# Two more rooms for the first expert table in batches 19 to 28

## The chip, the cores and the metric

The kernel runs on one core of a Trainium2 chip, in one launch. The metric is device time in microseconds (us). The kernel before was timed three times: 2976.99, 2976.50 and 2975.83 us, median 2976.5 us. The profile comes from one further execution.

## The reference, cut to what matters

Two transformer layers run over 256 tokens with 2048 features in float32; the change touches only the last part of the second, a layer of single-neuron experts (`peer`). Each token picks, for each of 8 heads, 16 of 16384 experts, and computes

```
u = jnp.take(expert_u, idx, axis=0)
a = jnp.einsum('thkd,td->thk', u, xb)
hid = jax.nn.gelu(a) * g
vsel = jnp.take(expert_v, idx, axis=0)
return jnp.einsum('thk,thkd->td', hid, vsel)
```

So there is a row of the first table (`expert_u`) to take, a dot product with the token's activations `xb`, a gate, and a row of the second table (`expert_v`) to add, 128 times for each token.

## The kernel before, in words

**Sparse and dense experts.** Of the 128 blocks of 128 experts, the last 40 are computed densely: their rows come as 40 panels of each table, 1 MB each, and TensorE multiplies all tokens by them (first table: `dense_u_panel`, second table: `dense_v_panel`). The other 88 blocks are sparse: their rows are gathered by index; an index that points into the dense blocks is out of bounds and moves no row.

**Gathers and rooms.** One gather takes 128 rows, one for each token of a half of the tokens, into a tile of 128 x 2048 floats (1 MB if no row were left out). There are 256 gathers of each table, numbered k = 0 to 255; four make a batch g = k // 4, 64 batches in all. Batches 0 to 31 serve the first 128 tokens, batches 32 to 63 the late rows (tokens 128 to 255). A tile of the first table goes into a room `s_u`, of the second table into a room `s_v`. There are 5 and 7 rooms; from batch 34 (`WIDE`) on 7 and 8. GpSimd (POOL) issues all gathers from one queue in one order: `gather_u(k)`, then `gather_v(k - 4)`. `gather_u(k)` waits until the last tile in its room has been used by a dot product (`dot_ready`), and `gather_v(k)` until TensorE has added the last tile in its room (`v_used`). Since the queue is in order, a gather that waits holds back all behind it.

**The other engines.** VectorE (DVE) computes `dot(k)`, two instructions on a room `s_u`. ScalarE (ACT) makes the gelu and the small matrices `s_spread`, and TensorE (PE) adds batch g's four `s_v` tiles (`adds`) one batch later. The first table's dense panels run on TensorE in batches 0 to 17, the last of them (panel 39) at the end of step 17. In steps 18 to 31, TensorE computes the gates of the dense experts, four tokens at a time (`token_four`, 64 of them: 8 each in steps 18 and 19, 4 each in 20 to 31), which counts `one_key_used`. The second table's dense panels run in steps 34 and later.

**The panel buffers.** Panels come through `s_raw0` and `s_raw1`, 8 KB per partition each, by DMAs that SyncE (SP) issues. Behind the last panel of the first table SP loads `s_xn_late` and `s_xres_late` (the late rows' activations and residual, 1 MB each, first needed in batch 32 and step 33), and then the first two panels of the second table (needed in step 34). Each of these waits for a count of `one_key_used`: 4, 8, 12 and 16. So between panel 39 and the second table's first panels, `s_raw0` and `s_raw1` hold nothing for a short time and then those panels.

Of the kernel before, what the change touches and what calls it, by code (L numbers as in the profile page):

```python
# [22 lines left out]
D = 2048  # L23
# [10 lines left out]
PH, TOPK, NKEYS = 8, 16, 128  # L34
SLOTS = PH * TOPK

DENSE = 40
# [9 lines left out]
NPANELS = sum(n for _, n in PANELS)  # L47
# [91 lines left out]
def four_of(g):  # L139

    if g < 4 * EARLY:
        return g % EARLY, g // EARLY
    if g < 4 * PH:
        g -= 4 * EARLY
        return EARLY + g % (PH - EARLY), g // (PH - EARLY)
    g -= 4 * PH
    return PH + g % PH, g // PH
# [38 lines left out]


WIDE = 34


def rooms_of(narrow, wide, start, tiles):

    rooms = []
    last, times = {}, [0] * wide
    later = list(range(narrow, wide)) + [(start + i) % narrow for i in range(narrow)]
    for k in range(tiles):
        r = k % narrow if k < start else later[(k - start) % wide]
        times[r] += 1
        rooms.append((r, times[r], last.get(r)))
        last[r] = k  # L200
    return rooms
# [42 lines left out]
def two_layers(nc, stream, dense_u, columns, x, meta, b_out, g_mix_post, g_ffn, g_ffn_post, g_norm1, g_norm2, w_forget,  # L244
# [5 lines left out]
    K, Q = 1024, 32  # L250
# [3 lines left out]
    def place(name, shape, offset, dt=f32):  # L254
        assert name not in names
        names.add(name)
        return nc.alloc_sbuf_tensor_at(name, shape, dt, offset=offset)
# [29 lines left out]
    ring0 = at  # L287
# [5 lines left out]
    S = at  # L293
# [60 lines left out]
    NE = len(panel_early)  # L354
    score = place("s_score", [128, TT * PH, 2 * NKEYS], S + 16 * K)
    NU, NV, NW, NH, BATCH, LAG = 5, 7, 4, 4, 4, 4
    ROUTES, GROUPS = TT * PH, TOPK // BATCH
    MU, MV = NU + 2, NV + 1
    u_room = rooms_of(NU, MU, WIDE * BATCH, ROUTES * TOPK)
    v_room = rooms_of(NV, MV, WIDE * BATCH, ROUTES * TOPK)  # L360


    ha = place("s_ha", [128, DENSE, T], S + 24 * K)
    u_slot = [place(f"s_u{i}", [128, D], before_group if i == 0 else ring0 + (1 + i) * 8 * K) for i in range(NU)]
    u_slot += [place("s_u5", [128, D], S + 0), place("s_u6", [128, D], S + 16 * K)]
    free = [S + 8 * K, ring0 - 8 * K, ring0 + 48 * K, ring0 + 56 * K, ring0 + 64 * K + (KT * L * 4),
            ring0 + 72 * K + (KT * L * 4), ring0 - 16 * K]
    v_slot = [place(f"s_v{i}", [128, D], free[i]) for i in range(NV)]
# [51 lines left out]
    with ExitStack() as ctx:  # L420
        bank = [ctx.enter_context(nc.psum_tensor(f"bank{b}", [128, 512], f32)) for b in range(8)]

        def sem(name):
            return ctx.enter_context(nc.semaphore(name))
# [5 lines left out]
        panel_used = sem("panel_used")  # L430
# [41 lines left out]
        one_key_ready, one_key_2_ready, one_key_used = sem("one_key_ready"), sem("one_key_2_ready"), sem("one_key_used")  # L472
# [6 lines left out]
        dot_ready, dots_added, gelu_ready, hid_ready = sem("dot_ready"), sem("dots_added"), sem("gelu_ready"), sem("hid_ready")  # L479
# [15 lines left out]
        @block.sync  # L495
        def _(sp):
            sp.dma_start(meta_sb[:, :], meta).then_inc(meta_loaded, 16)
            for t in range(TT):
                sp.dma_start(xres[:, t, :], x[t * 128:(t + 1) * 128, :]).then_inc(x_loaded[t], 16)
            sp.dma_start(cols[:, :], columns).then_inc(cols_loaded, 16)  # L500
            for s in range(4):
                sp.dma_start(raw[s][:, :], stream[s]).then_inc(raw_loaded[s], 16)
            panels = stream.rearrange("(q s) p n -> q s p n", s=4)
            with sp.Fori(1, NPANELS // 4) as q:
                for s in range(4):


                    sp.wait_ge(panel_used, q * 4 + (s - 4 + 1 + 1))
                    sp.dma_start(raw[s][:, :], panels[bass.ds(q, 1), s].rearrange("a p n -> (a p) n"))\
                        .then_inc(raw_loaded[s], 16)  # L510
            for d in range(NE, 2 * DENSE):
                if d == DENSE:
                    sp.wait_ge(panel_used, NPANELS + 1 + DENSE)
                    sp.wait_ge(one_key_used, 4)
                    sp.dma_start(xn_late[:, :], put_by[0]).then_inc(xn_back, 16)
                    sp.wait_ge(one_key_used, 8)
                    sp.dma_start(xres_late[:, :], put_by[1]).then_inc(xres_back, 16)
                if DENSE <= d < DENSE + 2:
                    sp.wait_ge(one_key_used, 12 + 4 * (d - DENSE))
                if d < NE + 2:  # L520
                    sp.wait_ge(split_ready, NSPLITS - 3 + d - NE)
                else:
                    sp.wait_ge(panel_used, NPANELS + 1 + d + 1 - 2)
                src = dense_u[d] if d < DENSE else expert_v[(SPARSE + d - DENSE) * NKEYS:(SPARSE + d - DENSE + 1) * NKEYS, :]
                r = (d - NE) % 2
                sp.dma_start(raw[r][:, :], src).then_inc(raw_loaded[r], 16)
            for t in range(TT):
                for q in range(4):
                    sp.wait_ge(out_ready, 4 * t + q + 1)
                    for c in range(4 if t == 0 else 2):  # L530
                        sp.dma_start(out[t * 128 + q * Q:t * 128 + (q + 1) * Q, c * 512:(c + 1) * 512],
                                     out_row[c * Q:(c + 1) * Q, t, q * 512:(q + 1) * 512]).then_inc(stored, 16)
            sp.wait_ge(stored, 16 * 16 * TT)
# [3 lines left out]
        def _(pool):  # L537
# [51 lines left out]
            for g, w in enumerate(POOL_WINDOWS):  # L589
                src, s = pin[:, 2 * g:2 * g + 2, :], 1  # L590
                own = src
# [28 lines left out]
            def gather_u(k):  # L620

                g, s = divmod(k, BATCH)
                th, j = four_of(g)
                slot = j * BATCH + s
                pool.wait_ge(expert_ready, th + 1)
                if k in (1, 2):
                    pool.wait_ge(split_ready, NSPLITS - 2 + k)
                if k in (3, 4):
                    pool.wait_ge(panel_used, NPANELS - 3 + k)
                r, _, last = u_room[k]  # L630
                if last is not None:
                    pool.wait_ge(dot_ready, last + 1)
                elif r == NU:
                    pool.wait_ge(dot_ready, PH * GROUPS * BATCH)
                elif r > NU:
                    pool.wait_ge(one_key_used, T // 4)
                index = bass.IndirectOffsetOnAxis(ap=u_index[th][:, slot:slot + 1], axis=0)
                pool.indirect_dma_start(u_slot[r][:, :], None, expert_u, index, bounds_check=SPARSE * NKEYS - 1,  # L638
                                        oob_is_err=False).then_inc(u_loaded[r], 16)

            def gather_v(k):

                g, q = divmod(k, BATCH)
                th, j = four_of(g)
                pool.wait_ge(v_index_ready, th + 1)
                if k == 0:
                    pool.wait_ge(late_stored, 32)
                if k == 4:
                    pool.wait_ge(xnt_ready, 1)
                if k == 6:  # L650
                    pool.wait_ge(res_taken, 1)
                r, _, last = v_room[k]
                if last is not None:
                    pool.wait_ge(v_used, last + 1)
                elif r >= NV:
                    pool.wait_ge(v_used, PH * GROUPS * BATCH + 1)
                index = bass.IndirectOffsetOnAxis(ap=v_index[th][:, q * GROUPS + j:q * GROUPS + j + 1], axis=0)
                pool.indirect_dma_start(v_slot[r][:, :], None, expert_v, index, bounds_check=SPARSE * NKEYS - 1,  # L658
                                        oob_is_err=False).then_inc(v_loaded[r], 16)

            gather_u(0)
            gather_v(0)
            gather_v(1)
            for k in range(1, ROUTES * TOPK + LAG):
                if k < ROUTES * TOPK:
                    gather_u(k)
                for first in {4: (2, 3), 5: (4, 5), 6: (6,)}.get(k, ()):
                    gather_v(first)
                if k >= LAG + NV:
                    gather_v(k - LAG)  # L670
# [1856 lines left out]
```

## Time and profile before

| | |
|---|---|
| median of three runs | 2976.5 us |
| the profiled execution's own time | 2973.8 us |
| its span in the profile | 2971.7 us |
| busy: TensorE, VectorE, ScalarE, GpSimd | 2759.5, 1917.5, 1177.4, 660.7 us |
| granted TensorE clock, mean | 0.948 of full speed |
| DMA, mean over the span | 264 GB/s |
| batches 0 to 63: first dot product to the last | 1851.1 to 2958.5 us |
| first dot product on the late rows (k = 128) | 2415.3 us |

The gathers fill the last 1100 us of the span. In the page's 40 slices (74.3 us each) the DMA engines are busy at 50 to 60% until then and at over 90% from slice 26 on. Times given as a place are counted from the start of the span.

### The profile page before, as it was taken

What the parts mean: (1) busy time and instruction counts of PE and PEld (TensorE: products, weight loads), DVE (VectorE), ACT (ScalarE), POOL (GpSimd) and SP (SyncE); (2) the same over time, 40 slices, a digit from 0 to 9 for tenths busy, and PEclk for the clock granted to TensorE, in tenths of its full rate; (3) what the DMA queues carried; (4) which work ended last, traced back from release to release, by engine and by line L of the source; (5) the groups of instructions that cost most, each with busy time, mean ns of one, the idle gap of its engine ahead of it and who ended that gap; (6) DMA issues with size and microseconds to landing.
All of it is one profiled execution on the core that took longest, in us unless ns stands there. A gap on an engine that the chain in (4) does not pass through costs nothing.

```text
span 2971.7 us, 45765 instructions
## 1 busy us (share of the span) xinstructions
PE 2759.5 (93%) x17115; PEld 2063.2 (69%) x17115; DVE 1917.5 (65%) x3302; ACT 1177.4 (40%) x2302; POOL 660.7 (22%) x568
## 2 busy tenths in 40 slices
PE   8999999999999997999999999999998787888885
PEld 7886778888888887989999889677764432222221
DVE  6888566655665556455444557988858885555556
ACT  1003443333333434434333445565556542223333
POOL 0000000000000000040000002454446665555554
PEclk9999999999999998999999999999996679989897
DMA  6432545555555553443455656999999999999998
GB/s 246 142 142 101 209 158 187 193 186 183 189 192 183 186 193 121 165 147 141 173 185 184 249 201 226 365 409 416 413 378 419 401 409 423 423 422 420 419 420 356
DMA packets 131299, 785.53 MB, mean 264 GB/s; under 512 B 34630, under 2 KB 34630, under 8 KB 35846
## 3 DMA queue, kind: packets, MB, share of 16 engines
q1 hardware_dynamic: 55040, 393.16, 36.0%
q0 software_dynamic: 75712, 389.74, 32.4%
q8 instruction: 94, 1.54, 0.2%
q14 instruction: 69, 0.57, 0.1%
q10 hardware_dynamic: 384, 0.52, 0.0%
HBM read 940.23 MB, written 4.19 MB: 318 GB/s over the span
## 4 chain that ended last, share of the span: by engine, by line
PE 62%; DMA 16%; DVE 12%; issue 6%; ACT 2%; POOL 2%; DVEq 1%; POOLq 0%; ACTq 0%
PE bank L1970 10%; PE bank L1964 10%; PE bank L1965 10%; PE bank L1966 10%; DMA s_u<-in_expert_u,s_u_index 10%; DMA s_v<-in_expert_v,s_v_index 6%; PE bank L2363 6%; PE bank L1971 5%; PE bank L2060 4%; DVE s_u L1824 3%; PE bank L2418 3%; PE bank L2373 2%; DVE s_cacc L1333 2%; POOL s_u L638 1%; DVE s_w_lo L1244 1%
## 5 line engine op out<-in xcount | busy, mean ns | idle before, releaser
L1244 DVE TENSOR_TENSOR s_w_lo<-s_raw,s_w_hi 128x2048 fp32r<-128x2048 f32 x258 | 592.6, 2297 | 577.0 <-ACT s_w_hi L685 576.5
L685 ACT ACTIVATE s_w_hi<-s_raw 128x2048 fp32r<-128x2048 f32 x256 | 490.4, 1916 | 750.6 <-PE bank L1966 475.2
L1970 PE MATMUL bank<-s_a,s_w_hi 128*128 128x512 f32 x1408 | 494.3, 394 | 3.2 <-DVE s_w_lo L1244 3.2
L1824 DVE CUSTOM_DVE_ANT_0 s_u<-s_u,s_xn_late 128x1024 f32<-128x1024 f32 x256 | 303.6, 1223 | 221.2 <-DMA s_u<-in_expert_u,s_u_index 195.3
L2418 PE MATMUL bank<-s_v,s_spread 128*32 128x512 f32 x2048 | 312.5, 727 | 142.2 <-DMA s_v<-in_expert_v,s_v_index 106.0
L1971 PE MATMUL bank<-s_a,s_w_lo 128*128 128x256 f32 x1408 | 395.1, 281 | 0.0
L638 POOL DMA_INDIRECT s_u<-in_expert_u,s_u_index x256 | 298.9, 1168 | 381.4 <-DVE s_halfdot L1824 222.4
L658 POOL DMA_INDIRECT s_v<-in_expert_v,s_v_index x256 | 311.5, 1217 | 206.6 <-PE bank L2418 120.3
L1824 DVE CUSTOM_DVE_ANT_0 s_u<-s_u,s_xn 128x1024 f32<-128x1024 f32 x256 | 303.0, 1223 | 46.6 <-DMA s_u<-in_expert_u,s_u_index 40.9
L1964 PE MATMUL bank<-s_a,s_w_hi 128*128 128x256 f32 x1152 | 325.1, 282 | 3.4 <-DVE s_a L1268 1.8
L1965 PE MATMUL bank<-s_a,s_w_hi 128*128 128x256 f32 x1152 | 324.4, 282 | 0.0
L1966 PE MATMUL bank<-s_a,s_w_lo 128*128 128x256 f32 x1152 | 324.0, 281 | 0.0
L1109 ACT ACTIVATE s_spread<-s_shifted,s_hid 32x32 f32<-32x32 f32 x784 | 249.4, 318 | 188.0 <-DVE s_hid L1873 169.0
L1970 PEld LDWEIGHTS bank<-s_a,s_w_hi 128*128 128x128 f32 x1408 | 264.7, 188 | 66.2 <-DVE s_w_lo L1244 6.4
L2418 PEld LDWEIGHTS bank<-s_v,s_spread 128*32 128x32 f32 x2048 | 64.0, 123 | 341.0 <-issue 284.6
L2373 PE MATMUL bank<-s_raw,s_ha 128*32 128x512 f32 x2560 | 297.1, 617 | 0.0
L2363 PE MATMUL bank<-s_xnt,s_raw 128*128 128x256 f32 x1184 | 265.2, 382 | 1.3 <-issue 0.9
L1971 PEld LDWEIGHTS bank<-s_a,s_w_lo 128*128 128x128 f32 x1408 | 264.9, 188 | 0.4
L2363 PEld LDWEIGHTS bank<-s_xnt,s_raw 128*128 128x128 f32 x1184 | 221.9, 190 | 59.6 <-issue 30.9
L2060 PE MATMUL bank<-s_a_f,s_raw 128*128 128x272 f32 x1024 | 235.2, 393 | 2.0 <-DVE s_a_f L1301 1.2
L2373 PEld LDWEIGHTS bank<-s_raw,s_ha 128*32 128x32 f32 x2560 | 94.8, 115 | 202.8 <-issue 202.0
L2060 PEld LDWEIGHTS bank<-s_a_f,s_raw 128*128 128x128 f32 x1024 | 194.4, 190 | 42.6 <-issue 2.6
(332 smaller groups left out, 3912.3 us busy)
## 6 DMA issues: line engine op xcount, KB each, us to landing
s_raw<-in_stream SPq DMA_DIRECT2D x292, 1024.0 KB, 4.8
s_raw<-in_expert_v SPq DMA_DIRECT2D x40, 1024.0 KB
s_raw<-in_dense_u SPq DMA_DIRECT2D x37, 1024.0 KB
s_u<-in_expert_u,s_u_index POOLq DMA_INDIRECT x256
s_v<-in_expert_v,s_v_index POOLq DMA_INDIRECT x256
s_panel_early<-in_dense_u POOLq DMA_DIRECT2D x3, 1024.0 KB, 11.4
s_xres<-in_x SPq DMA_DIRECT2D x2, 1024.0 KB, 5.9
out<-s_out_row SPq DMA_DIRECT2D x24, 64.0 KB
```

Source lines behind the costliest of these rows:

```text
L685: act.activation(w_hi[s % 2][:, :], raw[s][:, :], ACT.Copy).then_inc(hi_ready, 1)
L1244: dve.tensor_tensor(w_lo[s % 2][:, :], raw[s][:, :], w_hi[s % 2][:, :].bitcast(f32), ALU.subtract)\
L1824: ins = dve.tensor_tensor_reduce(out=u_slot[r][:, half], in0=u_slot[r][:, half], in1=xn_late[:, half] if t else xn[:, 0, half], scale=SHRI ...
L1964: pe.matmul(dst, left[0], right[0], start=start, stop=False)
L1965: pe.matmul(dst, left[0], right[1], start=False, stop=False)
L1966: return pe.matmul(dst, left[1], right[0], start=False, stop=stop)
L1970: pe.matmul(dst, left[0], both, start=start, stop=False)
L1971: return pe.matmul(dst[:, 0:T], left[1], both[:, 0], start=False, stop=stop)
L2060: ins = pe.matmul(bank[c][:, 0:L], raw[c % 4][:, k * 128:(k + 1) * 128], a_f[:, k, :], start=k == 0, stop=k == KT - 1)
L2363: ins = pe.matmul(bank[b][:, 0:T], source[:, k * 128:(k + 1) * 128], xnt[:, k, 0:T], start=k == 0, stop=k == KT - 1)
L2373: ins = pe.matmul(bank[4 * t + q][c * Q:(c + 1) * Q, :], ha[:, d, t * 128 + q * Q:t * 128 + (q + 1) * Q], raw[r][:, c * 512:(c + 1) * 512] ...
L2418: ins = pe.matmul(bank[4 * t + q][c * Q:(c + 1) * Q, :], spread[g % NW][:, q, :], v_slot[r][:, c * 512:(c + 1) * 512], start=False, stop=last)
```

## The change

`LENT = (19, 29)`: in batches 19 to 28 (k = 76 to 115) the first table has seven rooms. The two new ones, `s_u5` and `s_u6`, are the bytes of `s_raw0` and `s_raw1`. The two rooms that it has from batch 34 on are now called `s_u7` and `s_u8`. `rooms_of` now takes the open room whose last use is longest ago. The first gathers into the lent rooms, k = 76 and 77, wait until the first table's last dense panel is used (`panel_used`). On SP's queue the load of `s_xn_late` now waits for 24 groups of four tokens in place of 4, that of `s_xres_late` for 32 in place of 8, and the second table's first two dense panels wait for the last dot product in the lent rooms (k = 112 and 111) in place of 12 and 16 groups. The last gathers into the lent rooms are k = 111 and 112. Nothing is computed in another way or in another order on TensorE, VectorE or ScalarE.

```diff
+LENT = (19, 29)
-def rooms_of(narrow, wide, start, tiles):
+def rooms_of(stages, tiles):
     rooms = []
-    last, times = {}, [0] * wide
-    later = list(range(narrow, wide)) + [(start + i) % narrow for i in range(narrow)]
+    last, times = {}, {}
     for k in range(tiles):
-        r = k % narrow if k < start else later[(k - start) % wide]
-        times[r] += 1
+        open_rooms = [own for start, own in stages if start <= k][-1]
+        r = min(open_rooms, key=lambda own: last.get(own, -1))
+        times[r] = times.get(r, 0) + 1
         rooms.append((r, times[r], last.get(r)))
         last[r] = k
...
-    MU, MV = NU + 2, NV + 1
+    MU, MV = NU + 4, NV + 1
+    narrow = list(range(NU))
+    u_room = rooms_of([(0, narrow), (LENT[0] * BATCH, [NU, NU + 1] + narrow), (LENT[1] * BATCH, narrow),
+                       (WIDE * BATCH, [NU + 2, NU + 3] + narrow)], ROUTES * TOPK)
+    lent_until = [max(k for k in range(ROUTES * TOPK) if u_room[k][0] == NU + r) for r in range(2)]
...
+    u_slot += [place("s_u5", [128, D], ring0), place("s_u6", [128, D], ring0 + 8 * K)]
...
                 if d == DENSE:
                     sp.wait_ge(panel_used, NPANELS + 1 + DENSE)
-                    sp.wait_ge(one_key_used, 4)
+                    sp.wait_ge(one_key_used, 24)
                     sp.dma_start(xn_late[:, :], put_by[0]).then_inc(xn_back, 16)
-                    sp.wait_ge(one_key_used, 8)
+                    sp.wait_ge(one_key_used, 32)
                     sp.dma_start(xres_late[:, :], put_by[1]).then_inc(xres_back, 16)
                 if DENSE <= d < DENSE + 2:
-                    sp.wait_ge(one_key_used, 12 + 4 * (d - DENSE))
+                    sp.wait_ge(dot_ready, lent_until[(d - NE) % 2] + 1)
...
                 if last is not None:
                     pool.wait_ge(dot_ready, last + 1)
-                elif r == NU:
+                elif r in (NU, NU + 1):
+                    pool.wait_ge(panel_used, NPANELS + 1 + DENSE)
+                elif r == NU + 2:
```

GpSimd's queue at the start of batch 19, before: k = 75 of the first table (room 0, `s_u_133`), then k = 76 to 78 in rooms 1 to 3, with the second table's gathers between.

```order
L638 DMA s_u_133<-in_expert_u,s_u_index_187 128x2048 [waits dot_ready,expert_ready]
L658 DMA s_v_141<-in_expert_v,s_v_index_202 128x2048 [waits v_used,v_index_ready]
L638 DMA s_u_134<-in_expert_u,s_u_index_188 128x2048 [waits dot_ready,expert_ready]
L658 DMA s_v_142<-in_expert_v,s_v_index_203 128x2048 [waits v_used,v_index_ready]
L638 DMA s_u_135<-in_expert_u,s_u_index_188 128x2048 [waits dot_ready,expert_ready]
L658 DMA s_v_143<-in_expert_v,s_v_index_203 128x2048 [waits v_used,v_index_ready]
L638 DMA s_u_136<-in_expert_u,s_u_index_188 128x2048 [waits dot_ready,expert_ready]
```

The same place of the changed kernel, where `s_u_138` and `s_u_139` are the lent rooms.

```order
L645 DMA s_u_133<-in_expert_u,s_u_index_189 128x2048 [waits dot_ready,expert_ready]
L665 DMA s_v_143<-in_expert_v,s_v_index_204 128x2048 [waits v_used,v_index_ready]
L645 DMA s_u_138<-in_expert_u,s_u_index_190 128x2048 [waits panel_used,expert_ready]
L665 DMA s_v_144<-in_expert_v,s_v_index_205 128x2048 [waits v_used,v_index_ready]
L645 DMA s_u_139<-in_expert_u,s_u_index_190 128x2048 [waits panel_used,expert_ready]
L665 DMA s_v_145<-in_expert_v,s_v_index_205 128x2048 [waits v_used,v_index_ready]
L645 DMA s_u_134<-in_expert_u,s_u_index_190 128x2048 [waits dot_ready,expert_ready]
```

The order of tables is the same; k = 76 and 77 go to the lent rooms and wait for the dense panels, and k = 78 takes the room that k = 76 had.

SyncE's queue behind the first table's last panel, before: the late rows, then the second table's panels.

```order
L515 DMA s_xn_late<-put_by 128x2048 [waits one_key_used,panel_used]
L517 DMA s_xres_late<-put_by 128x2048 [waits one_key_used]
L526 DMA s_raw_66<-in_expert_v 128x2048 [waits panel_used,one_key_used]
L526 DMA s_raw_65<-in_expert_v 128x2048 [waits panel_used,one_key_used]
L526 DMA s_raw_66<-in_expert_v 128x2048 [waits panel_used]
```

The same place after.

```order
L520 DMA s_xn_late<-put_by 128x2048 [waits one_key_used,panel_used]
L522 DMA s_xres_late<-put_by 128x2048 [waits one_key_used]
L531 DMA s_raw_66<-in_expert_v 128x2048 [waits panel_used,dot_ready]
L531 DMA s_raw_65<-in_expert_v 128x2048 [waits panel_used,dot_ready]
L531 DMA s_raw_66<-in_expert_v 128x2048 [waits panel_used]
```

The order of the loads is the same; the two panels now wait for dot products.

## Rows read from the trace of the kernel before

**Rows 1.** The page: rate in each of 40 slices; the gathers' queue (packets, MB, share).

```profile
GB/s 246 142 142 101 209 158 187 193 186 183 189 192 183 186 193 121 165 147 141 173 185 184 249 201 226 365 409 416 413 378 419 401 409 423 423 422 420 419 420 356
...
q0 software_dynamic: 75712, 389.74, 32.4%
```

**Rows 2.** Windows: stretch, its length, busy us of PE, PEld, DVE, ACT, POOL; clock; DMA share; GB/s.

```profile
2200.00:2210.00 10.00, 8.49 (x48) 6.18 (x40) 4.37 (x11) 7.38 (x22) 5.28 (x5) 1.00 0.87 313
2210.00:2230.00 20.00, 17.98 (x114) 13.21 (x114) 13.50 (x27) 15.60 (x49) 8.98 (x8) 0.74 0.94 334
2230.00:2260.00 30.00, 23.88 (x152) 14.08 (x156) 27.07 (x57) 21.39 (x65) 17.99 (x16) 0.73 1.01 417
...
2290.00:2325.00 35.00, 27.67 (x154) 13.25 (x154) 29.63 (x58) 20.60 (x62) 25.42 (x20) 0.69 1.01 411
2325.00:2345.00 20.00, 18.42 (x106) 12.18 (x106) 17.09 (x36) 11.89 (x38) 12.08 (x12) 0.66 0.99 372
...
2370.00:2390.00 20.00, 18.21 (x106) 11.98 (x98) 17.19 (x34) 13.29 (x41) 13.37 (x12) 0.67 0.98 377
...
2440.00:2925.00 485.00, 406.07 (x3452) 122.76 (x3448) 275.28 (x559) 148.27 (x476) 267.32 (x226) 0.91 1.01 420
```

**Rows 3.** Windows of L638 alone (first table's gathers): busy (count), clock, share, GB/s.

```profile
1800.00:2201.00 401.00, 83.19 (x76) 1.00 0.95 378
```

**Rows 4.** The same of L1824 alone (dots, four records each).

```profile
1850.00:2357.00 507.00, 268.22 (x452) 0.91 0.99 397
```

**Rows 5.** Timeline of SyncE, 2180 to 2480: start, us, what.

```profile
2218.22 0.33 SPq L515 DMA_DIRECT2D s_xn_late<-put_by  x1
2228.17 0.33 SPq L517 DMA_DIRECT2D s_xres_late<-put_by  x1
2235.41 237.95 SPq L526 DMA_DIRECT2D s_raw<-in_expert_v  x5
```

**Rows 6.** Timeline of GpSimd; in brackets the idle time before and its releaser.

```profile
2199.70 1.63 POOL L658 DMA_INDIRECT s_v<-in_expert_v,s_v_index  x1 [6.97 <-PE bank L2418]
2201.63 0.99 POOL L638 DMA_INDIRECT s_u<-in_expert_u,s_u_index  x1 [0.30 <-PE bank L2418]
2202.93 0.99 POOL L658 DMA_INDIRECT s_v<-in_expert_v,s_v_index  x1 [0.30 <-issue]
2204.22 0.99 POOL L638 DMA_INDIRECT s_u<-in_expert_u,s_u_index  x1 [0.30 <-issue]
...
2220.89 1.07 POOL L658 DMA_INDIRECT s_v<-in_expert_v,s_v_index  x1 [6.05 <-PE bank L2418]
...
2238.13 1.11 POOL L658 DMA_INDIRECT s_v<-in_expert_v,s_v_index  x1 [2.38 <-DVE s_halfdot L1824]
...
2248.59 1.15 POOL L638 DMA_INDIRECT s_u<-in_expert_u,s_u_index  x1 [3.73 <-DVE s_halfdot L1824]
```

**Rows 7.** Timeline of TensorE: last dense panel, adds, fours of tokens.

```profile
2201.32 7.17 PE L2363 MATMUL bank<-s_xnt,s_raw 128*128 128x256 f32 x32
...
2235.31 5.93 PE L2418 MATMUL bank<-s_v,s_spread 128*32 128x512 f32 x32
...
2267.74 1.96 PE L2398 MATMUL bank<-s_one_key,s_one_key_more 128*128 128x40 f32 x16
...
2298.17 1.96 PE L2398 MATMUL bank<-s_one_key,s_one_key 128*128 128x40 f32 x16
```

**Rows 8.** Waits on GpSimd, 2180 to 2420: us in total, times, longest.

```profile
POOL s_u L638 <- DVE s_halfdot L1824: 37.8, 20, 4.0
...
POOL s_v L658 <- PE bank L2418: 13.3, 3, 7.0
```

**Rows 9.** Chain of waits, 2120 to 2480: gathers from issue to landing.

```profile
2261.11 12.96 DMA s_u<-in_expert_u,s_u_index
...
2374.32 14.59 DMA s_u<-in_expert_u,s_u_index
```

More of the change, by code:

```diff
@@ L357, in two_layers @@
     ROUTES, GROUPS = TT * PH, TOPK // BATCH
-    MU, MV = NU + 2, NV + 1
-    u_room = rooms_of(NU, MU, WIDE * BATCH, ROUTES * TOPK)
-    v_room = rooms_of(NV, MV, WIDE * BATCH, ROUTES * TOPK)
+    MU, MV = NU + 4, NV + 1
+    narrow = list(range(NU))
+    u_room = rooms_of([(0, narrow), (LENT[0] * BATCH, [NU, NU + 1] + narrow), (LENT[1] * BATCH, narrow),
+                       (WIDE * BATCH, [NU + 2, NU + 3] + narrow)], ROUTES * TOPK)
+    v_room = rooms_of([(0, list(range(NV))), (WIDE * BATCH, [NV] + list(range(NV)))], ROUTES * TOPK)
+    lent_until = [max(k for k in range(ROUTES * TOPK) if u_room[k][0] == NU + r) for r in range(2)]
     ha = place("s_ha", [128, DENSE, T], S + 24 * K)
     u_slot = [place(f"s_u{i}", [128, D], before_group if i == 0 else ring0 + (1 + i) * 8 * K) for i in range(NU)]
-    u_slot += [place("s_u5", [128, D], S + 0), place("s_u6", [128, D], S + 16 * K)]
+    u_slot += [place("s_u5", [128, D], ring0), place("s_u6", [128, D], ring0 + 8 * K)]
+    u_slot += [place("s_u7", [128, D], S + 0), place("s_u8", [128, D], S + 16 * K)]
     free = [S + 8 * K, ring0 - 8 * K, ring0 + 48 * K, ring0 + 56 * K, ring0 + 64 * K + (KT * L * 4),
@@ L632, in gather_u @@
                     pool.wait_ge(dot_ready, last + 1)
-                elif r == NU:
+                elif r in (NU, NU + 1):
+                    pool.wait_ge(panel_used, NPANELS + 1 + DENSE)
+                elif r == NU + 2:
                     pool.wait_ge(dot_ready, PH * GROUPS * BATCH)
-                elif r > NU:
+                elif r == NU + 3:
                     pool.wait_ge(one_key_used, T // 4)
```

## The prediction

> **What bounds the kernel now.** I read the page's slices first. From slice 26 on the DMA engines move 401 to 423 GB/s in nearly every slice, against 101 to 250 in the first 25 [rows 1]. Then I cut that stretch into windows. From 2440 to 2925 us the rate is 420 GB/s at a share of 1.01: there DMA bandwidth is the bound, and what is left to move at 2440 sets the end [rows 2]. Before 2440 there are two kinds of shortfall. From 2200 to 2230 the rate is 313 and 334 GB/s; this is where TensorE finishes the last dense panel and does double portions of token groups. From 2260 on it is near 420 but for two holes, 2325 to 2345 (372) and 2370 to 2390 (377), and a slight one at 2290 to 2325 (411) [rows 2]. So the account to keep is one of megabytes: every microsecond in which the engines move less than 420 GB/s before 2440 is paid at the end.
>
> Shortfall against 420 GB/s, in us: 2200 to 2210, 107/420 x 10 = 2.5; 2210 to 2230, 86/420 x 20 = 4.1; 2230 to 2260, 0.2; 2290 to 2325, 0.75; 2325 to 2345, 2.3; 2370 to 2390, 2.05. That is 6.8 us in the first part and 5.1 us in the later one: 11.9 us is all that a better supply of gathers could win.
>
> Why are there holes? GpSimd's queue waits for a free room. Between 2180 and 2420 it waited 37.8 us for dot products, that is for rooms of the first table, 20 times, and 13.3 us, 3 times, for rooms of the second [rows 8]. Two of those three are 6.97 us before 2199.70 and 6.05 us before 2220.89, 13.0 us together [rows 6], so from 2221 on the second table's rooms are named for hardly any wait.
>
> **The unit.** The gathers' queue moved 389.74 MB [rows 1]. Thirteen direct loads of 1.05 MB and a small one went by it too, so 512 gathers share some 376 MB: 0.734 MB each, 1.75 us at 420 GB/s. A panel or a late load is 1.05 MB, 2.5 us.
>
> **The waits at the start of the loan.** 76 gathers of the first table were issued before 2201 [rows 3], so k = 76 is the one at 2201.63 [rows 6]. It now waits for the last dense panel, which TensorE computes from 2201.32 for 7.17 us, to 2208.5 [rows 7]. Queued behind it are the second table's k = 72, the first's k = 77 and the second's k = 73, issued at 2202.93 and 2204.22 and after. All move back to about 2208.8, by 7 us. The next fixed point is the second table's gather at 2220.89, which waits for TensorE's adds of step 18, and the next the one at 2238.13 (its releaser is named as a dot product, but the adds of step 19 start at 2235.31 and fit as well) [rows 6, 7]. Between these the queue has room: 7 gathers at 1.3 us each fit between 2208.8 and 2218. So the 7 us are made up on GpSimd by 2221; the DMA engines meanwhile have one or two gathers left and run dry.
>
> **The loads that move.** Before, the two late loads went out at 2218.22 and 2228.17 and the second table's first panels from 2235.41 on (12 and 16 groups of tokens) [rows 5]; they filled the weak stretch. Now `s_xn_late` waits for the 24th group, done at 2267.74 + 1.96 = 2269.7, and `s_xres_late` for the 32nd, at 2300.1 [rows 7]. The two panels wait for dot product k = 112: 452 records at four each are 113 dot products by 2357 [rows 4]. All are in time for batch 32 and step 34, which start after 2415. So 4 x 1.05 = 4.2 MB, 10.0 us of DMA time, move from a stretch with slack into one with little.
>
> **What is delivered by 2260.** Before: 10 us x 313 + 20 x 334 + 30 x 417 = 22.3 MB, the 4.2 MB included [rows 2]. After: no more than was issued can arrive by 2239.6, and the fixed point at 2238.13 holds back the same second-table gathers as before. These are 8 of the first table (76 to 83) and 7 of the second (72 to 78), 15 x 0.734 = 11.0 MB, and 1.1 MB in flight at 2200, an estimate. From 2239.6 to 2260 GpSimd can issue one gather per 1.3 us, since the next wait for a dot product (3.73 us before 2248.59 [rows 6]) is for two products earlier now; so 20.4 us at 420 = 8.6 MB. Sum 20.7 MB, 1.6 MB less than before: **3.8 us lost**. Bounds: 10.0 us if no extra gather takes the place of the moved loads, and 0 if TensorE and VectorE, with less traffic beside them, free the rooms so that the weak stretch is filled as before.
>
> **What the two rooms give from 2260 on.** GpSimd is some 3 to 4 gathers ahead at 2260, and it has 7 rooms until k = 115 (some 2355). The slight shortfall (0.75) and the hole at 2325 (2.3) should close: 3.05 us. At the hole of 2370 the first table is back at five rooms, but 2.1 MB of panels, 5.0 us of work, were issued at 2357; I credit half of it, 1.0 us. **About 4.0 us gained**, between 0 and 5.1. VectorE does not stand against it: it is busy 29.63 of 35 us at 2290 [rows 2]. The new names of the rooms from batch 34 on cost nothing, since order and number are the same.
>
> The sum: 2973.8 (the profiled execution, 2.1 us around its span of 2971.7) + 3.8 - 4.0 = 2973.6. That execution stands 2.7 us under the median of the runs, so the forecast is 2976.3, rounded to 2976.0: **no change**.
>
> [...] In the hole the rate is 377 GB/s while a gather takes 14.59 us from issue to landing [rows 2, 9]; 14.59 us x 377 GB/s is 5.5 MB, 7.5 gathers in flight of the 12 rooms, and the engines are still not full. At 2261.11 it is 12.96 us [rows 9]. [...]
>
> **Rivals.**
> *The second table's rooms take over.* Slower. Place: GpSimd's `v_used` waits from batch 20 on. A gather of the second table stands between any two of the first, its seven rooms are as they were, and its tile is used one batch later. If GpSimd, once ahead, always stops there, gathers are delivered as before and the 4.2 MB are pure addition to the stretch 2260 to 2440: +10.0 us, less what of them falls into the holes (2 to 5.1 us): +5 to +8, 2981.5 to 2984.5. It decides as soon as those waits in 2240 to 2350 exceed some 10 us. For it: 13.3 us of such waits before. Against: none of weight after 2221 [rows 6, 8].
> *Depth buys nothing.* The holes come from GpSimd's and VectorE's pace and stay: +3.8, 2980.3. Against: 37.8 us of waits for dot products.
> *The weak stretch is filled after all.* Faster: of 11.9 us of shortfall all but the dry 4 us at 2201 goes: -8, 2968.5. For it: half of the shortfall lies there. Against: the fixed points at 2220.89 and 2238.13 are no rooms of the first table.
> *The loan does nothing and neither do the moved loads*: within 1 us; it can't be told from the forecast by the time, only by the waits.
>
> **How the numbers follow.** A measurement of this kernel tells 0.2% (6 us) from no change. Forecast 0.46, depth buys nothing 0.18, second table's rooms 0.18, weak stretch filled 0.18. The forecast's own range is 2972 to 2980. Beyond the 6 us lie most of the third and of the fourth case: slower 0.15, faster 0.16, same 0.69. The range runs from 2970 to 2983, which leaves the outer ends of both, 2 in 10.
>
> **What would show it.** Right: GpSimd idle for 6 to 7 us up to 2208.8 before k = 76, with DMA under 200 GB/s there; `s_xn_late` issued near 2270, `s_xres_late` near 2300, both panels near 2350; rates of 415 and more from 2290 to 2345; fewer waits of GpSimd for dot products in 2240 to 2360. Wrong: waits for TensorE's adds of 10 us or more there (second table's rooms), holes in the same places (depth), or dot product k = 128 earlier than 2415 by over 5 us with the same rate after 2440 (faster). A shift of more than 3 us that arises behind 2440 would break the account as such.

## The result, and the profile after

| | median, us | runs | against the kernel before in the same set |
|---|---|---|---|
| before | 2974.9 | 22 | |
| changed | 2979.78 | 22 | ratio 1.0016, 95% interval 1.001 to 1.0022; 4.9 us slower |

The forecast was 2976.0 us and no change. The time lies inside the range of 2970 to 2983 us, but the change is slower by more than its interval: small, under the 6 us that the prediction called the limit of what can be told, and told all the same by 22 runs of each kernel. The first three runs of the kernel before, on which the forecast stood, have a median of 2976.5 us; all 22 have 2974.9 us, so beside these the forecast itself stood 1.6 us too high. The profiled execution of the changed kernel took 2984.28 us, the longest of its 22; its first dot product starts at 1853.7 us, 2.6 us later than before, ahead of everything that was changed. All windows below are moved by such an offset (here 2.6 us), so that they begin as far behind the first dot product as those of before; where a view is not moved, the text says so.

The page of the changed kernel, GB/s in 40 slices and the gathers' queue; the same bytes as before [rows 1].

```profile
GB/s 246 141 142 99 204 163 185 191 188 183 190 190 184 190 188 127 159 152 139 176 183 183 240 201 238 371 409 414 413 358 406 409 402 423 423 421 420 418 417 350
...
q0 software_dynamic: 75712, 389.74, 32.3%
```

Windows of the kernel before, for all comparisons below (stretch, length, busy us of PE, PEld, DVE, ACT, POOL, clock, DMA share, GB/s). The stretch ahead of them, 2200 to 2210, and the one behind, from 2440, stand in [rows 2].

```profile
2210.00:2260.00 50.00, 41.87 (x264) 27.30 (x268) 40.57 (x83) 36.99 (x113) 26.97 (x24) 0.73 0.98 384
2290.00:2345.00 55.00, 46.09 (x260) 25.43 (x260) 46.72 (x93) 32.49 (x100) 37.50 (x31) 0.68 1.00 397
2345.00:2440.00 95.00, 71.20 (x418) 34.06 (x421) 76.74 (x149) 46.41 (x143) 62.86 (x54) 0.70 1.01 409
```

The same of the changed kernel, with the stretch ahead and the one behind.

```profile
2202.60:2212.60 10.00, 8.66 (x48) 6.26 (x40) 3.76 (x8) 7.38 (x22) 1.34 (x2) 1.00 0.38 144
2212.60:2262.60 50.00, 41.18 (x268) 26.82 (x272) 41.44 (x84) 37.96 (x115) 35.09 (x29) 0.74 0.95 365
2292.60:2347.60 55.00, 42.49 (x248) 23.32 (x241) 44.88 (x91) 32.31 (x100) 37.47 (x29) 0.69 1.01 412
2347.60:2442.60 95.00, 72.06 (x418) 36.24 (x418) 73.58 (x145) 44.13 (x136) 59.33 (x49) 0.67 1.00 401
2442.60:2927.60 485.00, 405.62 (x3444) 120.68 (x3440) 275.00 (x556) 144.90 (x467) 264.74 (x226) 0.90 1.01 420
```

Read as a shortfall against 420 GB/s (the rate of the last stretch, unchanged), in us, (420 - rate) / 420 x length. The four stretches are called A (2200 to 2210), B (2210 to 2260), C (2290 to 2345) and D (2345 to 2440); between B and C both kernels run at 423 GB/s:

| | A | B | C | D | sum |
|---|---|---|---|---|---|
| before | 2.5 | 4.3 | 3.0 | 2.5 | 12.3 |
| changed | 6.6 | 6.5 | 1.0 | 4.3 | 18.4 |

Up to 2260 the change costs 6.3 us. The two rooms win 2.0 us in C, and 1.8 us of that is gone in D. The sum is 6.1 us more, beside 4.9 us between the medians. The two profiled executions themselves lie 10.5 us apart, or 7.9 us without the 2.6 us at the start.

What stands in A: GpSimd's timeline of the changed kernel, with the idle time before each gather and its releaser. L665 is the second table's gather, L645 the first's, L2370 TensorE's dense panel.

```profile
2202.46 0.99 POOL L665 DMA_INDIRECT s_v<-in_expert_v,s_v_index  x1 [10.80 <-PE bank L2425]
2212.11 0.99 POOL L645 DMA_INDIRECT s_u<-in_expert_u,s_u_index  x1 [8.66 <-PE bank L2370]
2213.41 1.75 POOL L665 DMA_INDIRECT s_v<-in_expert_v,s_v_index  x1 [0.30 <-issue]
```

The gather k = 76 waits 8.66 us for the last dense panel, as the change says, where it had gone out 0.30 us behind its neighbour [rows 6]. Ahead of it the queue had waited 10.80 us for the adds, so that in 21 us one gather was issued, and the DMA engines ran at 144 GB/s. The 10.80 us are not the change's: two kernels below without loan or added wait show 10.55 and 10.35 us in this place, and A is at 334 and 341 GB/s in them. What empties A is the second wait on top.

SyncE's timeline of the changed kernel:

```profile
2271.37 0.33 SPq L520 DMA_DIRECT2D s_xn_late<-put_by  x1
2301.40 0.33 SPq L522 DMA_DIRECT2D s_xres_late<-put_by  x1
2360.53 129.59 SPq L531 DMA_DIRECT2D s_raw<-in_expert_v  x6
```

The late rows' loads went out at 2218.22 and 2228.17 before, the panels from 2235.41 [rows 5]. Now none of the four falls into B.

Waits on GpSimd from 2240 to 2360 in both kernels (not moved by the offset), before and then changed.

```profile
POOL s_u L638 <- DVE s_halfdot L1824: 14.4, 8, 3.7
...
POOL s_v L658 <- DVE s_halfdot L1824: 2.1, 1, 2.1
```

```profile
POOL s_v L665 <- PE bank L2425: 12.9, 3, 6.9
...
POOL s_v L665 <- DVE s_halfdot L1831: 6.6, 4, 5.6
...
POOL s_u L645 <- DVE s_halfdot L1831: 0.6, 2, 0.3
```

One of these waits, 5.6 us ahead of the gather at 2240.34, has its counterpart before ahead of the one at 2238.13, outside the view. With the window moved by 2.6 us the changed kernel's 6.6 us are 0.9. So the wait has changed its owner: 14.4 us for the first table's rooms became 0.6, and 2.1 us at the second table's gathers became 13.8 (12.9 + 0.9). The deeper side no longer waits; the other one does, for about as long.

### The profile page after: what moved, and what is told of

It is laid out like the page before. It is cut to its first block, busy times and chain, and to the rows that moved or that the text cites. A ratio compares the mean times of both kernels' runs of the same rounds, so it can differ in the third digit from the quotient of the medians.

```text
span 2982.2 us, 45765 instructions
## 1 busy us (share of the span) xinstructions
PE 2760.3 (93%) x17115; PEld 2063.4 (69%) x17115; DVE 1916.2 (64%) x3302; ACT 1177.5 (39%) x2302; POOL 662.9 (22%) x568
## 4 chain that ended last, share of the span: by engine, by line
PE 62%; DMA 17%; DVE 12%; issue 5%; ACT 2%; POOL 1%; DVEq 1%; POOLq 0%; SPq 0%; ACTq 0%
PE bank L1977 10%; PE bank L1971 10%; PE bank L1972 10%; PE bank L1973 10%; DMA s_u<-in_expert_u,s_u_index 9%; DMA s_v<-in_expert_v,s_v_index 8%; PE bank L2370 5%; PE bank L1978 5%; PE bank L2067 4%; DVE s_u L1831 3%; PE bank L2425 3%; DVE s_cacc L1340 1%; PE bank L2380 1%; PE bank L2405 1%; DVE s_w_lo L1251 1%
## 5 line engine op out<-in xcount | busy, mean ns | idle before, releaser
L665 POOL DMA_INDIRECT s_v<-in_expert_v,s_v_index x256 | 319.1, 1246 | 241.4 <-PE bank L2425 162.9
L645 POOL DMA_INDIRECT s_u<-in_expert_u,s_u_index x256 | 293.6, 1147 | 351.4 <-DVE s_halfdot L1831 189.0
L2370 PE MATMUL bank<-s_xnt,s_raw 128*128 128x256 f32 x1184 | 265.2, 382 | 1.7 <-DMA s_raw<-in_dense_u 1.7
L2370 PEld LDWEIGHTS bank<-s_xnt,s_raw 128*128 128x128 f32 x1184 | 222.2, 190 | 59.7 <-issue 30.9
## 6 DMA issues: line engine op xcount, KB each, us to landing
s_u<-in_expert_u,s_u_index POOLq DMA_INDIRECT x256, 20.7
s_v<-in_expert_v,s_v_index POOLq DMA_INDIRECT x256, 20.4
```

Source lines behind the costliest of these rows:

```text
L2370: ins = pe.matmul(bank[b][:, 0:T], source[:, k * 128:(k + 1) * 128], xnt[:, k, 0:T], start=k == 0, stop=k == KT - 1)
```

## The experiments

Each kernel was timed 11 times beside 33 runs of the kernel before on the same chip. The intervals reach some 2.7 us to either side, so two rows that differ by less than that are not told apart by their times alone. "Loan from 20 to 29" stands for `LENT = (20, 29)`: seven rooms from batch 20 on, five again from batch 29. The last column is the sum of the shortfall in A to D less that of before, each computed as above from the windows of its one profile. The edits without a loan are against the kernel before, the others against the changed kernel, where nothing else is said.

| kernel | median less before, us | ratio, 95% interval | A | B | C | D | shortfall less before |
|---|---|---|---|---|---|---|---|
| four loads late, no loan | +6.6 | 1.0020 (1.0011, 1.0029) | 2.0 | 9.9 | 1.8 | 2.9 | +4.3 |
| panels late, no loan | +0.4 | 1.0001 (0.9992, 1.0010) | 1.9 | 4.9 | 2.2 | 2.5 | -0.8 |
| loan 19 to 29, late rows early | +3.5 | 1.0010 (1.0001, 1.0020) | 6.2 | 3.8 | 1.6 | 3.8 | +3.1 |
| changed, loan from 20 | +6.2 | 1.0021 (1.0012, 1.0030) | 2.3 | 10.4 | 1.0 | 4.3 | +5.7 |
| wait of k = 76 alone | +2.7 | 1.0011 (1.0002, 1.0020) | 6.6 | 2.6 | 1.6 | 4.1 | +2.6 |
| loan 20 to 29, late rows early | +1.6 | 1.0005 (0.9996, 1.0014) | 2.6 | 5.4 | 1.0 | 4.8 | +1.5 |
| loan 20 to 32, late rows early | -0.3 | 1.0002 (0.9993, 1.0011) | 2.3 | 5.8 | 0.3 | 4.8 | +0.9 |
| loads one step earlier, no loan | -1.8 | 0.9996 (0.9986, 1.0005) | 2.0 | 2.7 | 2.5 | 2.9 | -2.2 |
| the same once more | -1.6 | 0.9994 (0.9985, 1.0003) | 1.8 | 2.5 | 2.2 | 4.5 | -1.3 |
| loads at once, no loan | -2.1 | 0.9993 (0.9984, 1.0002) | 1.6 | 1.0 | 3.8 | 3.8 | -2.1 |
| one room 20 to 31, panels early | -0.4 | 0.9996 (0.9987, 1.0005) | 2.3 | 3.3 | 0.4 | 5.7 | -0.6 |
| loan 20 to 32, late rows first | +0.7 | 1.0002 (0.9993, 1.0011) | 2.8 | 5.6 | 0.1 | 4.3 | +0.5 |

**The four loads late, without the loan**

```diff
-                    sp.wait_ge(one_key_used, 4)
+                    sp.wait_ge(one_key_used, 24)
...
-                    sp.wait_ge(one_key_used, 8)
+                    sp.wait_ge(one_key_used, 32)
...
-                    sp.wait_ge(one_key_used, 12 + 4 * (d - DENSE))
+                    sp.wait_ge(dot_ready, (112, 113)[(d - NE) % 2])
```

> Kernel before, rooms unchanged (5 for the first table until batch 34), but SyncE's four loads wait as in the changed kernel: the late rows' two for 24 and 32 groups of four tokens, the two panels for dot products 112 and 111. Theory A (the 4.2 MB taken out of the weak stretch 2200 to 2260 are the cost): slower by 6 to 9 us, more than the changed kernel's 4.9 us, since no lent room takes their place. Theory B (the wait of k = 76 for the last dense panel, which drains the DMA engines at 2201 to 2212, is the cost): within 1.5 us of the kernel before. Theory C (the return to five rooms at batch 29 is the cost): also no change.

6.6 us slower, as theory A said. Its windows A and B:

```profile
2203.50:2213.50 10.00, 8.49 (x48) 6.19 (x40) 3.90 (x9) 7.38 (x22) 4.64 (x5) 1.00 0.90 334
2213.50:2263.50 50.00, 42.39 (x280) 28.17 (x284) 43.90 (x89) 39.86 (x120) 30.91 (x25) 0.74 0.91 337
```

A is as before; in B the rate falls from 384 to 337 GB/s, 5.6 us, with no wait of k = 76 for the panel and no lent room. Moving the loads is enough to be as slow as the changed kernel.

**Only the panels late**

```diff
-                    sp.wait_ge(one_key_used, 12 + 4 * (d - DENSE))
+                    sp.wait_ge(dot_ready, (112, 113)[(d - NE) % 2])
```

> Kernel before, but only the two panels of the second table wait for dot products 112 and 111; the late rows' loads keep their waits for 4 and 8 groups. Theory A: half of the moved bytes, slower by 3 to 5 us. If all of the four loads' cost lies in the panels, which come when depth is lost, this is as slow as all four together. Theory B and C: no change.

No change (the interval ends at 3.0 us, where theory A's 3 to 5 began): theory A as it stood, by the number of bytes, does not fit this half of them. Window B has 379 GB/s against 384:

```profile
2211.00:2261.00 50.00, 42.85 (x280) 27.28 (x284) 43.69 (x89) 39.49 (x119) 29.79 (x26) 0.74 0.98 379
```

In 2230 to 2260 the engines run at 401 GB/s without the panels and at 417 with them. The late rows' loads are the ones that fall into the emptiest part, 2210 to 2230 [rows 2]: there the rate is 345 GB/s here and 275 in the kernel with all four loads late. The two kernels differ by these loads alone: 6.2 us between their medians, where 2.1 MB are 5.0 us.

**The loan with the late rows' loads early**

```diff
-                    sp.wait_ge(one_key_used, 24)
+                    sp.wait_ge(one_key_used, 4)
...
-                    sp.wait_ge(one_key_used, 32)
+                    sp.wait_ge(one_key_used, 8)
```

> Changed kernel, but the late rows' two loads wait for 4 and 8 groups again, as before the change; the panels stay late. Theory A: 2.1 MB come back into the weak stretch, so 2 to 5 us faster than the changed kernel, near the kernel before. Theory B: as slow as the changed kernel (4.9 us over the kernel before), since k = 76 waits all the same. Theory C: as slow as the changed kernel.

3.5 us over the kernel before: by the medians 1.4 us of the changed kernel's 4.9 go, fewer than theory A wanted and fewer than the times can tell, and 3.1 us more than the panels' lateness alone remain. The windows show where:

```profile
2203.40:2213.40 10.00, 9.15 (x52) 6.40 (x44) 3.26 (x6) 7.35 (x22) 0.99 (x1) 1.00 0.41 159
2213.40:2263.40 50.00, 41.15 (x268) 27.39 (x272) 41.67 (x86) 38.21 (x117) 36.25 (x29) 0.77 0.97 388
```

B is as good as before (388), A is at 159 GB/s. So a second cost sits in A.

**The changed kernel with the loan from batch 20**

```diff
-LENT = (19, 29)
+LENT = (20, 29)
```

> Changed kernel with the loan from batch 20 (k = 80) instead of 19, so that the first lent gathers come after the last dense panel and do not wait for it. Theory B: 4 us or more faster than the changed kernel, at or under the kernel before. Theory A: as the changed kernel within 1.5 us, since what is delivered by 2240 is limited by the second table's rooms in any case. Theory C: no change against the changed kernel.

No faster than the changed kernel (6.2 against 4.9 us over the kernel before), though the wait in A is gone. Its windows A and B:

```profile
2200.90:2210.90 10.00, 8.65 (x48) 6.26 (x40) 3.76 (x8) 7.38 (x22) 4.79 (x5) 1.00 0.87 324
2210.90:2260.90 50.00, 42.22 (x276) 28.76 (x280) 42.53 (x85) 39.15 (x119) 32.37 (x26) 0.72 0.88 333
```

A has 324 GB/s again, B has 333 where the changed kernel had 365. With the late loads missing, A and B together fall short by 12.7 us here and by 13.1 us with the wait; if the wait does not empty A, B is emptier. That is theory A's answer, and it seemed to clear the wait. The next kernel shows that this was too quick.

**The wait of k = 76 alone**

```diff
+                if k == 76:
+                    pool.wait_ge(panel_used, NPANELS + 1 + DENSE)
                 if last is not None:
```

> Kernel before, with one wait more: GpSimd waits before k = 76 for the last dense panel of the first table. No room is lent and no load moved. Theory D (this wait drains the DMA engines and costs whenever the late rows' loads are there to fill the rest of the weak stretch): 3.0 us slower, as the loan with the late rows' loads early stands to its kernel with the panels late alone (3.5 - 0.4 us). Theory E (the wait is made up by 2221, as the prediction said): within 1 us of the kernel before.

2.7 us slower, with nothing else changed: theory D. Windows A and B:

```profile
2201.80:2211.80 10.00, 8.06 (x44) 6.04 (x36) 4.32 (x10) 7.36 (x22) 1.25 (x2) 1.00 0.38 142
2211.80:2261.80 50.00, 39.77 (x243) 26.49 (x243) 36.77 (x74) 33.91 (x104) 29.23 (x26) 0.70 0.99 398
```

A loses 4.1 us, B makes up 1.7 with the late loads in it. So the two costs do not seem to add. Where the late rows' loads are early, the wait costs 2.7 us, and 2.4 us more shortfall in A and B. Where they are late, the kernel with the wait (the changed one) and the one without (loan from 20) differ by -1.3 us in time and 0.4 us in A and B. By the times alone, -1.3 against 2.7 us, this is likely and not shown. Together with the four loads late (6.6) the sum would be 9.3 us; the changed kernel has both and is 4.9 us slower, the loan with them.

**The loan without either cost**

```diff
-LENT = (19, 29)
+LENT = (20, 29)
...
-                    sp.wait_ge(one_key_used, 24)
+                    sp.wait_ge(one_key_used, 4)
...
-                    sp.wait_ge(one_key_used, 32)
+                    sp.wait_ge(one_key_used, 8)
```

> Changed kernel without its two costs as theory D sees them: loan from batch 20 instead of 19 (no wait for the last dense panel), late rows' loads at 4 and 8 groups. Theory D: 3 us faster than the loan from 19 with the same loads (which was 3.5 us over the kernel before), so within 1.5 us of the kernel before. Theory F (the loan itself costs, by the room's return at batch 29 or by the second table's rooms): still 3 us or more over the kernel before.

1.6 us over the kernel before, with an interval that holds no change, and 1.9 us under the loan from 19 in the differences to before. Theory D wanted 3 and within 1.5: close to it. It is less than theory F's 3 us over the kernel before, though the interval, up to 4.2 us, does not exclude them. There is no gain either. The fair partner of this kernel is the one with only the panels late (+0.4 us), which has the same loads, its panels some 9 us later, and no loan: the loan adds 1.2 us to it. To the kernel with all four loads late (+6.6) the loan from 20 (+6.2) adds -0.4 us. In neither pair do the rooms buy time. Its windows C and D:

```profile
2291.10:2346.10 55.00, 45.04 (x264) 25.85 (x260) 46.18 (x92) 34.10 (x104) 37.41 (x30) 0.69 1.01 412
2346.10:2441.10 95.00, 71.62 (x401) 36.47 (x405) 72.22 (x142) 41.25 (x128) 58.74 (x51) 0.66 0.99 399
```

C rises from 397 to 412 GB/s and D falls from 409 to 399: 2.0 us won, 2.3 us lost.

**The loan until batch 32**

Against the kernel of the section before:

```diff
-LENT = (20, 29)
+LENT = (20, 32)
```

> As the loan from batch 20 to 29 with the late rows' loads early, but the rooms go back only at batch 32, and the two panels wait for the last dot product in them (k near 126, some 2415 us; they are needed near 2441). Theory G (the gain of the rooms at 2290 to 2345, some 1.5 to 2 us, is given back at the return, 2370 to 2415): 1.5 to 3 us faster than the loan to 29, so 1 to 3 us under the kernel before. Rival: the panels come too late for step 34 and TensorE waits for them, or the return costs the same, only later: no faster than the loan to 29.

0.3 us under the kernel before by the medians, 1.0002 by the ratio: no change. Against the loan to 29 it is 1.9 us better in the differences, inside what theory G asked and less than two such times can tell, but D is no better, only C:

```profile
2290.70:2345.70 55.00, 42.58 (x264) 22.05 (x260) 47.21 (x94) 34.20 (x104) 40.17 (x33) 0.75 1.01 418
2345.70:2440.70 95.00, 72.61 (x397) 37.88 (x389) 71.30 (x140) 41.13 (x127) 56.06 (x48) 0.66 0.99 399
```

So the return at batch 29 is not shown to be what empties D.

**The loads one step earlier, no loan, twice**

```diff
-                    sp.wait_ge(one_key_used, 4)
                     sp.dma_start(xn_late[:, :], put_by[0]).then_inc(xn_back, 16)
-                    sp.wait_ge(one_key_used, 8)
+                    sp.wait_ge(one_key_used, 4)
                     sp.dma_start(xres_late[:, :], put_by[1]).then_inc(xres_back, 16)
...
-                    sp.wait_ge(one_key_used, 12 + 4 * (d - DENSE))
+                    sp.wait_ge(one_key_used, 8 + 4 * (d - DENSE))
```

> Kernel before, each of SyncE's four loads one step earlier: the late rows' first right after the last dense panel, the second at 4 groups, the panels at 8 and 12. No loan. If the account by megabytes holds, this fills more of the weak stretch 2208 to 2230: 1 to 3 us faster than the kernel before. Rival: the loads come ahead of gathers that VectorE and TensorE need in steps 18 and 19, and what they gain is lost there: no change or slower.

> The same kernel as with the loads one step earlier (1.8 us under the kernel before, its interval reaching over no change), once more, to tell whether it is faster: again 1 to 3 us under the kernel before if the account holds, 0 plus or minus 1 us if the first result was chance.

1.8 and 1.6 us under the kernel before. Each interval reaches just over no change, so that it is faster is likely and not shown. The two profiles of this one kernel differ by 1.6 us in D (2.9 and 4.5), which is how far one profile can be trusted there. B rises to 397 GB/s in the first:

```profile
2211.10:2261.10 50.00, 42.64 (x276) 28.77 (x280) 42.40 (x85) 38.91 (x118) 28.90 (x25) 0.75 0.99 397
```

**Both late loads at once**

```diff
-                    sp.wait_ge(one_key_used, 4)
...
-                    sp.wait_ge(one_key_used, 8)
...
-                    sp.wait_ge(one_key_used, 12 + 4 * (d - DENSE))
+                    sp.wait_ge(one_key_used, 4 + 4 * (d - DENSE))
```

> Kernel before, the late rows' two loads both right after the last dense panel, the second table's two panels at 4 and 8 groups; no loan. Account by megabytes: at least as fast as with the loads one step earlier (1.8 us under the kernel before), so 2 to 4 us under the kernel before. Rival: 2.1 MB in one go stand before the gathers of k = 78 on and step 19 waits for them: no faster than the kernel before.

2.1 us under the kernel before, again with an interval up to 1.0002. A and B are nearly full (3.3 us less shortfall in B than before), but C and D have 2.1 us more. Whether what is filled early opens again later, one profile does not tell.

**One room lent, panels early**

```diff
-LENT = (19, 29)
+LENT = (20, 31)
...
-    MU, MV = NU + 4, NV + 1
+    MU, MV = NU + 3, NV + 1
...
-    u_slot += [place("s_u5", [128, D], ring0), place("s_u6", [128, D], ring0 + 8 * K)]
+    u_slot += [place("s_u5", [128, D], ring0 + 72 * K)]
...
-                    sp.wait_ge(one_key_used, 24)
                     sp.dma_start(xn_late[:, :], put_by[0]).then_inc(xn_back, 16)
-                    sp.wait_ge(one_key_used, 32)
+                if DENSE <= d < DENSE + 2:
+                    sp.wait_ge(one_key_used, 4 + 4 * (d - DENSE))
+                if d == DENSE + 2:
+                    sp.wait_ge(dot_ready, lent_until + 1)
                     sp.dma_start(xres_late[:, :], put_by[1]).then_inc(xres_back, 16)
-                if DENSE <= d < DENSE + 2:
-                    sp.wait_ge(dot_ready, lent_until[(d - NE) % 2] + 1)
...
```

The lent room is the place of `s_xres_late`, so that load alone waits until the room is free again.

> One room is lent to the first table in batches 20 to 30, from the place of the late rows' residual, so that both panels and the other late load stay early (right after the last dense panel; panels at 4 and 8 groups) and only the residual's 1.05 MB waits until the room is given back, near 2400. Account by megabytes: 1.05 MB less in the weak stretch (2.5 us lost against all loads early), 1.5 to 2 us won by the deeper room in 2290 to 2345: within 1.5 us of the kernel before. If the rooms' depth is worth more than that with the panels in early: 2 to 4 us faster.

0.4 us under the kernel before: no change, as the account said. The two panels are issued from 2219.66 on here, and D falls short by 5.7 us, the most of all.

**The loan to 32 with the late rows first**

```diff
-LENT = (19, 29)
+LENT = (20, 32)
...
-                    sp.wait_ge(one_key_used, 24)
                     sp.dma_start(xn_late[:, :], put_by[0]).then_inc(xn_back, 16)
-                    sp.wait_ge(one_key_used, 32)
+                    sp.wait_ge(one_key_used, 4)
```

> The loan from batch 20 to 32 with the late rows' loads one step earlier still (none and 4 groups). If both effects add: 1 to 2 us faster than the same loan with 4 and 8 groups (0.3 us under the kernel before), so 1.5 to 2.5 us under the kernel before. If the return of the rooms at batch 32 takes all: as the kernel before.

0.7 us over the kernel before. The two effects do not add; with and without the earlier loads the longer loan shows no gain. Nor do the earlier loads fill B here: 5.6 us of shortfall against 5.8 with the loads at 4 and 8 groups. C is all but full (0.1), and D has 4.3.

## Why the prediction was right or wrong

*What bounds the kernel*: right. Behind 2440 the rate is 420 GB/s in both kernels, and in all thirteen profiles of changed kernels (one kernel twice) the shortfall up to 2440 follows the difference of the medians: largest deviation 2.3 us (the four loads late), the others within 1.2 us. Against the time of the profiled execution itself, less its offset, the account is within 2.1 us each time. It can't be much sharper: one GB/s more or less in the 485 us behind 2440, where the profiles read 419 to 421, is 1.2 us.

*The limit of what can be told* was put at 6 us; 22 runs of each tell about 2 us (the interval is 1.8 us to either side). "No change" stood on a sum of -0.2 us, +3.8 and -4.0, where the runs showed a change. The terms were the error, not the limit: the first by 2.5 us, the second by 3.8.

*The waits at the start of the loan*: wait and place right (k = 76 at 2212.11 for the dense panel; foreseen 2208.8 plus the offset of 2.6), and wrong in what follows. "The 7 us are made up on GpSimd by 2221" is true of the queue: the trace has the second table's next gather that waits for adds at 2223.41, 2.5 us later than before, which is the offset. It is not true of the DMA engines, which do not get back the time that they pass empty: alone the wait costs 2.7 us. The sum priced it only inside what is delivered by 2260, and up to 2240 that was right: 12.1 MB foreseen, 12.0 measured.

*What is delivered by 2260*: a step that failed by size. The prediction had 20.7 MB after against 22.3 before, 3.8 us. Measured: 10 x 144 + 50 x 365 = 19.7 MB, 6.3 us. The 20.4 us from 2239.6 on, set at 420 GB/s since GpSimd could issue a gather each 1.3 us, are what failed: 384 GB/s in the 20 us from 2242.6 in the changed kernel, 7.7 MB against 8.6. GpSimd's queue had stood for 5.6 us until 2240.34; the rate was 329 and 311 GB/s in the two stretches of 5 us from 2237.6 on, and 400 only from 2247.6, though the queue did not stand again. The prediction gave the engines their full rate as soon as gathers went out.

*The loads that move*: the bytes were priced together. The panels cost nothing clear of noise (+0.4 us), the late rows' loads 6.2 us more.

*What the rooms give*: the step that failed by most. 2.0 us in C, where 3.05 were foreseen, and -1.8 us in D, where +1.0 was. Together 0.2 in place of 4.0 us. Kernels with the loan have C + D between 4.4 and 6.1 us, those without between 4.7 and 7.6, the kernel before 5.5. C is 0.1 to 1.6 us with the loan and 1.6 to 3.8 without, D 3.8 to 5.7 with it and 2.5 to 4.5 without: the loan goes with less shortfall in C and more in D, and does not remove it. In the changed kernel the first table is back at five rooms in D, and GpSimd waits there for dot products:

```profile
2365.34 0.99 POOL L645 DMA_INDIRECT s_u<-in_expert_u,s_u_index  x1 [3.82 <-DVE s_halfdot L1831]
...
2371.52 0.98 POOL L645 DMA_INDIRECT s_u<-in_expert_u,s_u_index  x1 [3.90 <-DVE s_halfdot L1831]
...
2377.71 0.99 POOL L645 DMA_INDIRECT s_u<-in_expert_u,s_u_index  x1 [3.91 <-DVE s_halfdot L1831]
```

These waits are no mark of the return, though. In D they come to 24.5 us here and 14.6 before, but to 28.0 and 24.6 us in the kernels with all four loads late and with the panels late, which have five rooms throughout and fall short by only 2.9 and 2.5 us in D. The loan to 32, too, has no smaller shortfall in D (4.8 us), and the kernel that lent one room has the largest (5.7) with its panels early, so neither the return at batch 29 nor the two panels issued late is needed for it. What sets D stays open. The clock granted to TensorE there is 0.66 to 0.72 of full speed in all kernels; two profiles of one kernel have 0.72 with 2.9 us of shortfall and 0.66 with 4.5, but the kernel with the four loads late has 0.67 with 2.9, so the clock alone does not order them.

*The rivals.* "The second table's rooms take over" named the wait that did appear (13.8 us at its gathers in the window moved by the offset, 19.5 in the one that is not, over the 10 us that were to decide) and the sign; its price of 5 to 8 us was near. It got a chance of 0.18. That this wait costs time is not shown: the loan from 20, with 14.5 us of it, is no slower than its partner without a loan, which has none. Its argument, 4.2 MB as pure addition, is not what happened, as the panels show. So its nearness is in part luck. "Depth buys nothing" came out nearest in time (2980.3 against 2979.8) and in sum, not in mechanism: with more depth C is fuller, at 408 to 419 GB/s in the kernels with the loan against 391 to 408 in those without. "The weak stretch is filled after all" did not happen.

## What to carry to other kernels

Where DMA bandwidth bounds the end, keep an account of the megabytes that are not moved before the bound stretch begins, stretch by stretch: the difference of two such accounts gave the difference in time to about 1 us in twelve of thirteen cases here, and to 2.3 us in the other. A load that fills an empty stretch is worth its full time there and costs that time if it is moved into a full one (6.2 us for two loads here, where 20 us without them ran at 275 GB/s), while a load in a stretch that is nearly full without it can be moved at little cost (0.4 us for two panels, where 30 us without them ran at 401 GB/s); price each load by the rate at the place that it leaves. A room added to one of two streams that share an in-order queue can hand the wait to the other stream, as here: 14.4 us became 0.6 and 2.1 became 13.8.

## What the runs showed that was not expected

GpSimd's queue, held for 8.65 us by the wait of k = 76 alone, was back at the next wait for adds by 2221.85, and the hold cost DMA time all the same: 4.1 us of shortfall in A, and 2.7 us at the end (0.6 to 6.0 by the interval). Two costs in the same stretch probably do not add: 2.7 us and 6.6 us alone, 4.9 us for both with the loan. And the loan without either of them is 1.6 us over the kernel before and not a gain.
